# The combine stage of a two-block transformer kernel: who multiplies the gathered expert sums by the gate, and who adds the residual

## The reference, cut to what matters

```
h = modulate(rms_norm(x, norm2_g), shift2, scale2)
y = zeros; y[slot_tok] += out            # weighted sums of the experts' outputs, per token
x = x + gate2 * y
return rms_norm(x, final_norm_g)
```

## Time and profile before

| what | us |
|---|---|
| median of 3 runs | 2924.6 |
| lowest and highest of them | 2921.72, 2927.68 |
| the profiled execution's own time | 2927.36 |
| its span, first to last instruction | 2925.6 |

### The profile page before, as it was taken

The page is one execution under the profiler, slowest core; times in us unless marked ns, Lnnn a source line. Parts: engine busy times, 40 slices in busy tenths (PEclk is TensorE's granted clock), DMA queues, the critical chain, the costliest instruction groups (busy, mean ns, idle before and its releaser), DMA issues. The chain is left out here.

```text
span 2925.6 us, 37705 instructions
## 1 busy us (share of the span) xinstructions
PE 2801.6 (96%) x14123; PEld 2265.7 (77%) x14123; DVE 1845.2 (63%) x2990; ACT 1285.9 (44%) x2032; POOL 440.7 (15%) x258
## 2 busy tenths in 40 slices
PE   7999998999999999899999999999999998999999
PEld 4766675778887778577988888888878767888886
DVE  6365787778778577836555122544431348999997
ACT  4355634542223243434444212222211236999995
POOL 1000020000000000011000222212122112544443
PEclk9999999999999999999999999999999998999999
DMA  6000064564445757323101212110222225777774
GB/s 254 30 23 16 9 246 156 188 221 163 165 145 195 285 195 283 132 103 113 33 24 62 78 70 102 43 44 34 102 72 75 104 103 214 262 269 267 257 264 169
DMA packets 116407, 407.32 MB, mean 139 GB/s; under 512 B 23556, under 2 KB 29988, under 8 KB 104736
## 3 DMA queue, kind: packets, MB, share of 16 engines
q1 hardware_dynamic: 82104, 348.82, 32.6%
q10 hardware_dynamic: 16440, 39.98, 3.7%
q0 software_dynamic: 17712, 16.52, 2.6%
HBM read 402.05 MB, written 82.66 MB: 166 GB/s over the span
## 5 line engine op out<-in xcount | busy, mean ns | idle before, releaser
L662 PE MATMUL psum<-ff_g,ffo_w_split 128*128 128x512 f32 x1056 | 247.2, 395 | 10.4 <-POOLq L799 5.9
L662 PEld LDWEIGHTS psum<-ff_g,ffo_w_split 128*128 128x128 f32 x1056 | 199.5, 190 | 53.6 <-POOLq L568 6.3
L4239 DVE TENSOR_TENSOR ex_g_lo<-ex_g_raw,ex_g_hi 128x1024 fp32r<-128x1024 f32 x188 | 221.0, 1217 | 0.8 <-ACT ex_g_hi L4176 0.7
L1045 PE MATMUL psum<-fi_t_sum_hi,fi_w_sum 128*128 128x512 f32 x704 | 220.3, 389 | 0.0
L4176 ACT CAST ex_g_hi<-ex_g_raw 128x1024 fp32r<-128x1024 f32 x188 | 192.0, 1053 | 1.5 <-PE psum L4119 1.5
L1045 PEld LDWEIGHTS psum<-fi_t_sum_hi,fi_w_sum 128*128 128x128 f32 x704 | 132.2, 188 | 27.4
L4117 PE MATMUL psum<-ex_g_hi,ex_x_hi 128*128 128x512 f32 x376 | 150.9, 401 | 0.0
L4119 PE MATMUL psum<-ex_g_hi,ex_x_lo 128*128 128x512 f32 x376 | 147.1, 391 | 0.0
L4118 PE MATMUL psum<-ex_g_lo,ex_x_hi 128*128 128x512 f32 x376 | 147.1, 391 | 0.0
L1045 PE MATMUL psum<-fi_t_sum_lo,fi_w_sum 128*128 128x512 f32 x352 | 137.1, 389 | 0.0
L1104 ACT CAST fi_w_sum<-fi_sum 128x512 fp32r<-128x512 f32 x88 | 54.4, 622 | 173.7 <-PE psum L1045 105.9
(11 more groups left out here) (659 smaller groups left out, 7561.0 us busy)
## 6 DMA issues: line engine op xcount, KB each, us to landing
ex_g_raw<-in_w_experts_gu_dram SPq DMA_DIRECT2D x32, 2048.0 KB, 8.5
ex_d_raw<-in_w_experts_d_dram SPq DMA_DIRECT2D x32, 1024.0 KB, 8.6
fi_raw<-in_ffn_in_dram SPq DMA_DIRECT2D x22, 1024.0 KB, 5.3
ffo_w_raw<-in_ffn_out_dram SPq DMA_DIRECT2D x31, 704.0 KB, 6.3
wom_w<-in_mod_w_dram SPq DMA_DIRECT2D x8, 2048.0 KB, 8.1
fi_first_raw<-in_ffn_in_dram SPq DMA_DIRECT2D x22, 512.0 KB, 4.5
ff_g<-fi_g SPq DMA_DIRECT2D x43, 256.0 KB, 2.0
ml_raw<-in_w_ml_dram SPq DMA_DIRECT2D x16, 512.0 KB, 5.1
```

The source lines that it names most:

```text
L662: mm = nc.tensor.matmul(chip.psum[:, 2 * u + h, :], w[:, v % 2, k * P:(k + 1) * P], (a[u] if isinstance(a, tuple) else a)[:, c * n_kc + k, ...
L1045: mm = mm_(self.result(name, j), w[:, part, k * P:(k + 1) * P], a[:, k, :], start=(k == 0 and p3 == 0), stop=(k == 3 and p3 == 2))
L4239: nc.vector.tensor_tensor(cols(g_lo, n), cols(raw.g_raw[i % 3], n), cols(g_hi, n).bitcast(F32), ALU.subtract).then_inc(q["g_lo_made"], 1)
```

## The change

For tiles 4 to 7 GpSimd no longer adds x. It multiplies the gathered sum by the gate itself, as soon as the tile's load has landed. TensorE adds x for those tiles too, by the same two fp32 matmuls as for tiles 0 to 3. VectorE scales only tiles 0 to 3, and its four other scales fall out of its list. The loads are issued in the order 0, 4, 1, 2, 5, 3, 6, 7 in place of 4, 0, 1, 5, 2, 6, 3, 7. The semaphores `to_add` and `added` are replaced by one, `by_pool`, on which TensorE waits ahead of the earlier blocks of tiles 4 to 7.

```diff
-    ADDED = (4, 5, 6, 7)
+    BY_POOL = (4, 5, 6, 7)
...
     def on_sp(self, sp):
         sp.wait_ge(self.ready, 1)
-        for i in (4, 0, 1, 5, 2, 6, 3, 7):
+        for i in (0, 4, 1, 2, 5, 3, 6, 7):
             sp.dma_start(self.tile(i), self.sums_dram[i * P:(i + 1) * P, :]).then_inc(self.e_in[i], 16)
...
     def on_pool(self, pool):
-        for n, i in enumerate(self.ADDED):
-            pool.wait_ge(self.to_add, n + 1)
-            self.chip.nc.gpsimd.tensor_tensor(self.tile(i), self.tile(i), self.x_tm[:, i, :], ALU.add).then_inc(self.added, 1)
+        for n, i in enumerate(self.BY_POOL):
+            pool.wait_ge(self.e_in[i], 16)
+            self.chip.nc.gpsimd.tensor_tensor(self.tile(i), self.tile(i), self.gate_r[:], ALU.mult).then_inc(self.by_pool, 1)
...
         for n, i in enumerate((4, 5)):
             pe.wait_ge(self.made, n + 1)
-            self.last_block(pe, i, True)
-            pe.wait_ge(self.added, n + 1)
+            self.residual(pe, i)
+            self.last_block(pe, i)
+            pe.wait_ge(self.by_pool, n + 1)
             self.earlier_blocks(pe, i)
         pe.wait_ge(self.scaled, 4)
         self.earlier_blocks(pe, 3)
         for n, i in enumerate((6, 7)):
             pe.wait_ge(self.made, n + 3)
-            self.last_block(pe, i, True)
-            pe.wait_ge(self.added, n + 3)
+            self.residual(pe, i)
+            self.last_block(pe, i)
+            pe.wait_ge(self.by_pool, n + 3)
             self.earlier_blocks(pe, i)
...
-        scale(4)
         scale(0)
         scale(1)
-        scale(5)
         scale(2)
+        scale(3)
         dve.wait_ge(self.fin_in, 16)
         finish(0)
         finish(1)
-        scale(6)
         finish(2)
-        scale(3)
-        scale(7)
         finish(4)
```

More of the change, by code:

```diff
@@ L4322, in __init__ @@
         self.fin_in, self.ready, self.counted, self.ids_made, self.hot_made, self.o_made, self.o_hi_made, self.o_lo_made, \
-            self.scaled, self.to_add, self.added, self.mixed, self.summed, self.var, self.root, self.made, self.out_done = \
+            self.scaled, self.by_pool, self.mixed, self.summed, self.var, self.root, self.made, self.out_done = \
             (chip.sem("co_" + n) for n in ("fin_in", "ready", "counted", "ids_made", "hot_made", "o_made", "o_hi_made",
-                                           "o_lo_made", "scaled", "to_add", "added", "mixed", "summed", "var", "root", "made",
+                                           "o_lo_made", "scaled", "by_pool", "mixed", "summed", "var", "root", "made",
                                            "out_done"))
@@ L4363, in residual, with last_block @@
                                        start=True, stop=False)
-    def last_block(self, pe, i, start):
+    def last_block(self, pe, i):
         hot = self.hot[:, i * P:(i + 1) * P]
@@ L4368, in last_block @@
             part = slice(s * HALF, (s + 1) * HALF)
-            self.chip.nc.tensor.matmul(self.bank(i, s), hot, self.o_hi[:, part], start=start, stop=False)
+            self.chip.nc.tensor.matmul(self.bank(i, s), hot, self.o_hi[:, part], start=False, stop=False)
             self.chip.nc.tensor.matmul(self.bank(i, s), hot, self.o_lo[:, part], start=False, stop=False)
@@ L4386, in on_pe @@
         for i in (0, 1, 2):
-            self.last_block(pe, i, False)
+            self.last_block(pe, i)
         pe.wait_ge(self.o_made, 1)
         self.residual(pe, 3)
-        self.last_block(pe, 3, False)
+        self.last_block(pe, 3)
         for i in (0, 1, 2):
@@ L4435, in scale @@
             v.tensor_tensor(self.tile(i), self.tile(i), self.gate_r[:], ALU.mult)\
-                .then_inc(self.to_add if i in self.ADDED else self.scaled, 1)
+                .then_inc(self.scaled, 1)
         def finish(i):
```

## The result

The changed kernel takes 2931.86 us (median of 20 runs, 2926.54 to 2937.26), the kernel before 2925.59 (20 runs, 2920.7 to 2930.26). The ratio is 1.002 with a 95% interval of 1.0014 to 1.0026: 6.3 us by the medians, 4.1 to 7.6 by the interval. 2930.9 was forecast, with 2927 to 2935 as the range.

The account below looks back on a forecast made before the run. TensorE was taken as the bound in the last 35 us. Residuals +6.88, lost wait for scale 3 -0.98 and late y of tile 0 +0.43 give +6.3 on the median 2924.6: 2930.9 us, range 2927 to 2935.

Parts of the forecast that it names:

- The bound: Last 35 us: TensorE runs matmuls back to back from 2901 to 2919.61, its only wait 0.98 us for scale 3.
- Four residuals at 6.88: TensorE, tiles 4 to 7: each added residual costs two fp32 matmuls, 1.72 us, with nothing hiding them; +6.88 us.
- The wait for scale 3 at -0.98: TensorE before tile 3's earlier blocks: its wait for VectorE's scale of tile 3 goes, -0.98 us.
- y of tile 0 late, +0.43: VectorE's finish 0, queued behind blocked scale 3, makes y at 2906.45, not 2905.94; TensorE waits before tile 4, +0.43 us.
- the load's landing, taken to go by place: Loads land by place in the queue, not by tile: tile 5, fifth, at 2901.5; tile 3, sixth, at 2902.8.
- The second value of the forecast: The sum without the late y of tile 0: +5.9 us in place of +6.3; chance 0.3.
- GpSimd's multiply at 2.38: GpSimd, tiles 4 to 7: a multiply costs 2.38 us like an add of the same shape, ends 2.36 and 4.09.
- The rule of taking turns: GpSimd multiplies and VectorE scales take turns, the later one waiting for the whole of the other; a finish is not held.
- The chances that it adds up for "the same": Chance that the whole time counts as unchanged within 0.2% (5.85 us): added up to 0.34, then stated as 0.36.
- cover for the residuals: Rival: VectorE's list sets the end and residuals fill TensorE's slack; -0.5 us, 2924.1; chance 0.05.
- a clock fall: Rival: the clock falls to 1.2 GHz from 2906 on, doubling 19.2 us of matmuls; about +25, 2950; chance 0.03.
- multiplies that hold VectorE longer: Rival: multiply 6 passes scale 3 (+8.7, 2933.3), or a multiply takes 4.09 us (+9.3, 2933.9); chance 0.12.

Follow-up runs that it names:

- none, two and four: The changed kernel with none, two or all four of TensorE's added residuals for tiles 4 to 7: stage 23.12, 26.55 and 29.99 us.
- no residuals: The changed kernel without TensorE's four added residuals, x left out for tiles 4 to 7: stage 23.12 us, whole time 1.0001 of before.
- scale 3 early: The kernel before with scale 3 moved ahead of finish 2 and scale 7 behind finish 4 on VectorE: stage 23.10 us, whole time 0.9996 of before.
- the run with the residuals alone: The kernel before with four residuals added on TensorE and nothing else changed: stage 29.99 us, whole time 1.0021 of before.
- the old load order: The changed kernel with its loads back in the order 4, 0, 1, 5, 2, 6, 3, 7: stage 31.83 us, 1.84 over the changed kernel.

## Why the prediction was right

**The bound.** TensorE without a gap from 2901 to the last tile, with one wait of 0.98 for scale 3: shown. Removing that wait alone gave -1.02, and each residual added its full 1.72 at none, two and four of them.

**Four residuals at 6.88.** Measured 6.87, by taking them out. Nothing hid them.

**The wait for scale 3 at -0.98.** Measured -1.00 (no residuals) and -1.02 (scale 3 early). In the changed kernel it vanishes because scale 3 is early; in the run with the residuals alone it vanishes because TensorE is late. Both leave +5.87.

**y of tile 0 late, +0.43: this term was mis-sized, it measured 0.** The step that failed is the load's landing, taken to go by place. The load in fifth place took 8.5 to 8.9 us in the six traces with the old order of the loads and 7.6 to 8.0 in the three with the new one. I put tile 5 at 2901.5 and so multiply 5's end at 2903.9. In the changed kernel multiply 5 started at 2899.60, which is 2901.05 in the times of before, and tile 3 had landed at 2901.16, which is 2902.61 there. Scale 3 was blocked for 0.79 us (2901.16 to 2901.95) instead of 1.1, and with the earlier landing it ended 0.5 us sooner than forecast and held finish 0 for 0.1 us at most. In the times of before, y of tile 0 was made at 2905.94, the very time of before, and TensorE was free at 2906.15, as forecast. The second value of the forecast, +5.9 without this term, is what happened. The mechanism behind it is real, as the old load order shows with 1.84 us; the new load order leaves it a margin of about 0.2 us (y made at 2904.49, TensorE's next residual at 2904.70).

**GpSimd's multiply at 2.38.** Measured 2.35, and TensorE never waited for one. The add of 2.38 that served as the price was not without a scale beside it, as the prediction has it: scale 3 came upon it (2.16 us in the chain, ending at 2912.28), and it was the scale that waited.

**The rule of taking turns.** Scales beside a multiply took 1.38 to 2.52 us in place of 1.21, a y from PSUM kept 1.28, and scale 3 ended 1.08 us after the multiply that blocked it, here as with the old load order. The Trainium skill (SBUF — State Buffer, section Who interferes with whom) has a VectorE instruction with two SBUF inputs contend with a GpSimd instruction that reads SBUF; the runs agree with it. Whether a second multiply would pass a scale that is already waiting was not put to the test: multiply 6 began 0.50 us after multiply 5 had ended, when its load landed, and no run shows a scale and a second multiply, its load landed, both waiting at the end of a multiply.

**The whole time.** 5.87 us in the stage against 6.3 by the medians, inside the interval of 4.1 to 7.6; I know of nothing outside the stage that the edit should change. That the medians differ by the forecast's own 6.3 is luck, since 0.43 of it was not there. That the changed kernel takes longer is clear of noise; whether by more than the 0.2% that the prediction counted as slower is not, for the interval of 1.0014 to 1.0026 lies on both sides of it. The chances that it adds up for "the same" come to 0.37, not 0.34 (0.17 + 0.15 + 0.05). The rivals: cover for the residuals is ruled out by the runs with none, two and four; a clock fall by the windows; multiplies that hold VectorE longer did not occur with the new load order: the four took 2.35 to 2.8 us, and multiply 6's load came too late for it to pass scale 3, so that form of the rival stays untested.

## What to carry to other kernels

An engine can be as busy as its neighbour and not be the bound: VectorE was busy for over 85% of the windows, but only 0.98 us of it ended on TensorE, so in this stage relief for VectorE could not be worth more than that, while each us put on TensorE counted in full. Before moving work, add up the waits of the receiving engine in that stage; what does not fit in them lengthens the stage. And in an in-order list look at what stands behind an instruction that waits for a load: moving scale 3 ahead of one finish (-1.02) was worth as much as all that the edit does for VectorE, four scales taken off included (-1.00).

## What the hardware showed that I had not expected

Eight loads of one size in one queue did not land evenly, and the uneven place moved. From issue to landing the third and the fifth took 5.5 and 8.6 us in the kernel before, 6.4 and 8.0 in the changed one, with the first at 3.7 and the last at 10.7 and 10.6 in both. The loads of the changed kernel, third and fifth in the queue (issue; then size and us to landing):

```profile
2890.54 0.43 SPq L4345 DMA_DIRECT2D co_e<-expert_sums  x1
...
co_e<-expert_sums SPq DMA_DIRECT2D x1, 512.0 KB, 6.4
...
2891.49 0.52 SPq L4345 DMA_DIRECT2D co_e<-expert_sums  x1
...
co_e<-expert_sums SPq DMA_DIRECT2D x1, 512.0 KB, 8.0
```

A pause in the landings stood ahead of the fifth load before and ahead of the third after. The nine traces tell part of it apart: the fifth took 8.5 to 8.9 us in all six with the old order, two of which are the changed kernel but for the order and the place of scale 3, and 7.6 to 8.0 in all three with the new one, so it goes with the order of the loads. The third took 5.5 to 6.4 under the old and 5.6 to 6.4 under the new. What sets either was not tried. By these figures, a forecast that hangs on one such landing should carry a spread of about one us.
